# A two-layer streaming encoder trunk on one core: who normalises the second head of each latent attention unit

## The reference, cut to what matters

```python
s = (einsum('bqhl,bkl->bhqk', q_lat, c_kv) + einsum('bqhr,bkr->bhqk', q_rope, k_rope)) * MLA_SCALE
visible = (k_pos[None, :] // CHUNK) <= (q_pos[:, None] // CHUNK)      # CHUNK = 64
p = softmax(where(visible, s, -inf), axis=-1)
o = einsum('bhqk,bkl->bqhl', p, c_kv)
```

## Time and profile before

| | |
|---|---|
| median of three executions | 1850.35 us (1850.24 to 1850.81) |
| the profiled execution | 1849.15 us |
| its span in the profile | 1847.4 us |
| instructions | 33704 |
| TensorE busy | 1824.8 us (99%) |
| VectorE busy | 923.5 us (50%) |
| ScalarE busy | 559.5 us (30%) |
| GpSimd busy | 1075.4 us (58%) |
| granted TensorE clock | 1.0 of full in both attention stages |

### The profile page before, as it was taken

The page is one execution under the profiler, slowest core; times in us unless marked ns, Lnnn a source line. Parts: engine busy times, 40 slices in busy tenths (PEclk is TensorE's granted clock), DMA queues, the critical chain, the costliest instruction groups (busy, mean ns, idle before and its releaser), DMA issues.

```text
span 1847.4 us, 33704 instructions
## 1 busy us (share of the span) xinstructions
PE 1824.8 (99%) x14214; PEld 1768.4 (96%) x14214; DVE 923.5 (50%) x1634; ACT 559.5 (30%) x1197; POOL 1075.4 (58%) x996
## 2 busy tenths in 40 slices
PE   9999999999999999999999999999999999999999
PEld 8999889999999999999999998899999999999999
DVE  6666775232755532523556767752336555235143
ACT  4444443112422211202344445430133222112021
POOL 8686534656555555557665864446456555555564
PEclk9999999999999999999999999999999999999999
DMA  5242112233222222223343421222422222222222
GB/s 189 88 132 86 54 42 84 88 120 112 72 90 92 84 89 92 86 80 97 99 143 93 127 87 47 70 66 84 152 81 75 86 92 89 84 92 91 79 86 95
DMA packets 76231, 170.49 MB, mean 92 GB/s; under 512 B 6384, under 2 KB 34160, under 8 KB 76080
## 3 DMA queue, kind: packets, MB, share of 16 engines
q1 hardware_dynamic: 68752, 160.79, 27.1%
q10 hardware_dynamic: 7328, 7.54, 1.2%
HBM read 156.41 MB, written 9.79 MB: 90 GB/s over the span
## 4 chain that ended last, share of the span: by engine, by line
PE 92%; DVE 5%; ACT 1%; POOL 1%; issue 1%; DMA 0%; SPq 0%; DVEq 0%; ACTq 0%; POOLq 0%
PE ps L1579 76%; PE ps L1614 3%; PE ps L1742 2%; PE ps L1700 2%; DVE xn L1101 1%; DVE xT L1446 1%; DVE mix L1443 1%; PE ps L1796 1%; PE ps L1653 1%; PE ps L1802 1%; DVE R L1101 1%; PE ps L1719 1%; DVE xT L1264 1%; PE ps L1668 1%; PE ps L1738 1%
## 5 line engine op out<-in xcount | busy, mean ns | idle before, releaser
L1579 PE MATMUL ps<-xn,wsp 128*128 128x272 f32 x7824 | 1002.0, 289 | 5.7 <-issue 2.2
L1579 PEld LDWEIGHTS ps<-xn,wsp 128*128 128x128 f32 x7824 | 986.1, 189 | 10.8 <-issue 6.0
L616 POOL CAST wsp<-raw 128x1024 fp32r<-128x1024 f32 (+2 forms) x222 | 220.1, 997 | 505.0 <-DMA raw<-in_wstream 450.3
L623 POOL TENSOR_TENSOR wsp<-raw,wsp 128x1024 fp32r<-128x1024 f32 (+2 forms) x278 | 492.1, 1782 | 16.2
L1579 PE MATMUL ps<-R,wsp 128*128 128x272 f32 x3840 | 486.2, 288 | 0.1
L1579 PEld LDWEIGHTS ps<-R,wsp 128*128 128x128 f32 x3840 | 482.7, 188 | 1.2 <-DVE xT L1130 0.5
L610 POOL TENSOR_TENSOR wsp<-raw,wsp 128x256 fp32r<-128x256 f32 x304 | 235.5, 795 | 12.2
L605 POOL CAST wsp<-raw 128x512 fp32r<-128x512 f32 x152 | 112.2, 738 | 147.9 <-DMA raw<-in_wstream 113.3
L1101 DVE SCALAR_TENSOR_TENSOR R<-ps,R 64x256 fp32r<-64x256 f32 (+12 forms) x264 | 130.0, 510 | 73.2 <-ACT R L753 24.6
L1462 DVE TENSOR_TENSOR mix<-ps,rstd 128x272 f32<-128x272 f32 x88 | 38.8, 441 | 202.9 <-PE ps L1579 192.6
L986 ACT ACTIVATE mix<-vv 128x2 f32<-128x2 f32 x88 | 17.9, 204 | 363.0 <-DVE mix L1464 363.0
(11 more groups left out here) (230 smaller groups left out, 1529.2 us busy)
## 6 DMA issues: line engine op xcount, KB each, us to landing
raw<-in_wstream SPq DMA_DIRECT2D x233, 512.0 KB, 3.5
raw<-in_wstream SPq DMA_DIRECT2D x48, 128.0 KB, 2.6
raw<-in_wstream SPq DMA_DIRECT2D x16, 384.0 KB, 3.0
raw<-in_kc SPq DMA_DIRECT2D x8, 512.0 KB, 3.8
raw<-in_vc SPq DMA_DIRECT2D x8, 512.0 KB, 4.8
xT<-in_x_in SPq DMA_DIRECT2D x8, 272.0 KB, 5.3
out_k_out<-mix ACTq DMA_DIRECT2D x8, 272.0 KB, 2.9
xT<-in_x_in SPq DMA_DIRECT2D x1, 2176.0 KB, 9.2
```

Of the source, the lines that this page charges most:

```text
L616: ins = nc.gpsimd.tensor_copy(dst[:, 0, f], part[:, f])
L623: ins = nc.gpsimd.tensor_tensor(dst[:, 1, f], part[:, f], dst[:, 0, f].bitcast(F32), ALU.subtract)
L1579: mm = pe.matmul(z[:, h], w[:, x, (k0 + k) * P:(k0 + k + 1) * P], rhs[:, y, k, h * HT:(h + 1) * HT], start=(k == 0 and (x, y) == (0, 0)), ...
```

## The change

The first head is normalised by VectorE as before. For the second head VectorE makes the reciprocal alone and raises `p_scaled`; ScalarE, which has just made the exponents, waits for that and writes the head's normalised exponents itself, with a `Copy` whose scale is the reciprocal. In all it counts three steps of `p_scaled` a unit in place of two, and TensorE's waits are renumbered. The M units are as they were but for the count.

```diff
@@ exponents (ScalarE), after the two Exp
+                        act.wait_ge(S["p_scaled"], 3 * (s - NS) + 2)
+                        ac(pr_view(s, w)[:, 1], z_view(s, w)[:, 1], ACT.Copy, scale=rsum[:, 2 * i + 1:2 * i + 2]).then_inc(S["p_scaled"], 1)
@@ normalise (VectorE), M unit
-                                            ALU.mult).then_inc(S["p_scaled"], 2)
+                                            ALU.mult).then_inc(S["p_scaled"], 3)
@@ normalise (VectorE), m unit
-                        for r in range(2):
-                            dve.wait_ge(S["e_done"], 2 * (s - NS) + r + 1)
-                            link(v.reciprocal(rsum[:, 2 * i + r:2 * i + r + 1], rsum[:, 2 * i + r:2 * i + r + 1]))
-                            v.tensor_scalar(pr_view(s, w)[:, r], z_view(s, w)[:, r], rsum[:, 2 * i + r:2 * i + r + 1], None,
-                                            ALU.mult).then_inc(S["p_scaled"], 1)
+                        dve.wait_ge(S["e_done"], 2 * (s - NS) + 1)
+                        link(v.reciprocal(rsum[:, 2 * i:2 * i + 1], rsum[:, 2 * i:2 * i + 1]))
+                        v.tensor_scalar(pr_view(s, w)[:, 0], z_view(s, w)[:, 0], rsum[:, 2 * i:2 * i + 1], None,
+                                        ALU.mult).then_inc(S["p_scaled"], 1)
+                        dve.wait_ge(S["e_done"], 2 * (s - NS) + 2)
+                        v.reciprocal(rsum[:, 2 * i + 1:2 * i + 2], rsum[:, 2 * i + 1:2 * i + 2]).then_inc(S["p_scaled"], 1)
@@ turn (TensorE)
-                            pe.wait_ge(S["p_scaled"], 2 * (n - NS) + 2)
+                            pe.wait_ge(S["p_scaled"], 3 * (n - NS) + 3)
-                                pe.wait_ge(S["p_scaled"], 2 * (n - NS) + r + 1)
+                                pe.wait_ge(S["p_scaled"], 3 * (n - NS) + (3 if r else 1))
```

## The result

The changed kernel takes 1856.95 us (median of six, 1855.58 to 1858.31) where the kernel before, measured beside it, takes 1850.30 (1850.02 to 1851.57). The ratio is 1.0035, 95% interval 1.0025 to 1.0045: slower by 6.6 us. Measured once more with the experiments it was 1855.42 and 1855.98 against 1850.39, ratios 1.0026 (1.0016 to 1.0036) and 1.0025 (1.0012 to 1.0038), so 5.0 to 5.6 us. Forecast were 3.25 us, so 1853.6, in a range that ended at 1855.2. The side was right, the size too small.

What follows compares the result with a forecast made beforehand. TensorE, busy 1824.8 of 1847.4 us, was taken as the bound, so only its waits count. A 2.22 + B 1.03 + C 0 = 3.25 us over the median of 1850.35 gave 1853.6 us, range 1850.9 to 1855.2.

Steps and rivals of the forecast that it cites:

- A: Steps 27 and 28: late value tile vv 1 makes TensorE wait at pv, 1.11 us a layer, 2.22 together.
- B: Steps 20 to 23: scores of step 23 start late, 0.45 us in layer 0 and 0.58 in layer 1, 1.03 together.
- The walk: All 16 units of a layer reckoned by latest input; three tight places, 3.25 us in all, chance 0.60.
- the first bank wait: Step 22: the ql tile waits for the bank ot holds, 216.35 for 216.19; B without the collision is 0.5.
- that first shift: Step 20: the kv eviction puts the chain back by 0.6 us; claimed swallowed in layer 0 by GpSimd holding line 1301.
- The second head's probabilities are ready at the same moment: Every changed unit: probabilities ready at the same moment or up to 0.1 us sooner, no TensorE wait, worth nothing.
- C: Step 29, kv 3: 0.55 us a layer later but covered by the wait for GpSimd, so 0; uncovered 1.1 us.
- The sum: A 2.22, B 1.03 and C 0 give 3.25 us of added TensorE waits.
- Hidden: Rival: TensorE feels nothing, as copies are cheaper or VectorE, with less work, catches up; 1850.4 us, chance 0.14.
- Slower: Rival: GpSimd holds the port through both subtractions, B 2.4 us, 1855.0 us; chance 0.12 including lost cover in C.
- the copy's price: ScalarE's new copy, priced like a sigmoid with scale: 0.48 us at 256 columns, 0.58 at 384, 0.69 at 512.

Runs made afterwards that it cites:

- e5: Changed kernel, but VectorE scales the second head again while ScalarE still waits for the second reciprocal at the same place; 1851.81 us, ratio 1.0004.
- r_after_2: Repeat of the changed kernel with nothing altered, profiled again; 1855.98 us, ratio 1.0025.
- e6: Changed kernel, but in step 22 VectorE writes the maxima to PSUM and the multiplication reads them there; 1855.42 us, ratio 1.0024.
- e3b: Kernel before, with ScalarE's copy in steps 20, 21, 22, 27 and 28 alone, 10 copies of 32; 1855.67 us, ratio 1.0028.
- e4: Changed kernel, with each of the 32 copies placed behind its step's evictions in ScalarE's queue; 1851.20 us, ratio 1.0003.
- e11: Changed kernel, with weight tiles CR 1 and CR 0 exchanged in the stream; 1855.64 us, ratio 1.0026 to the kernel before.
- r_before_1: Repeat of the kernel before with nothing altered, profiled; 1851.24 us, ratio 1.0003 against itself.
- e7: Kernel before, with three tiles moved to other steps (vv 1 to 27, kv 3 to 26, ot 1 to 23); 1857.06 us.
- e8: Changed kernel, with vv 1 moved to step 27, kv 3 to 26 and ot 1 to 23; 1859.50 us.
- e9: Changed kernel, with ScalarE's copy behind the evictions and weight tiles CR 1 and CR 0 exchanged; 1847.39 us, ratio 0.9980 to the kernel before.
- e10: Kernel before, with weight tiles CR 1 and CR 0 exchanged in the stream; 1848.06 us, ratio 0.9986.

## Why the prediction was wrong

**A** was right in mechanism and order, and 16% short: 1.32 us a layer for 1.11. The chain itself came out as reckoned: the exponents 0.63 late and the low parts of `vv` 1.57 late, both beyond the 1.75 us by which TensorE was behind already, the copies 0.474 and 0.581 us in the mean for 0.48 and 0.58. But TensorE started 0.26 us after the low part had ended, and not 0.05 as at lines 1799 and 1805. In e5 the same instruction started 0.26 us late too. Line 1745 has several waits in front of it; but in step 22 it started 0.09 us after its last input. The cause stays open.

**B**, the chain from step 20 to step 23, is the step that failed: 2.65 us where the prediction had 1.03 (2.5 and 2.0 in the two later profiles). Three things in it:
- The walk stopped at the scores of step 23. The `ql` tile of step 22 holds the bank of the next `pv` 0. I had the first bank wait, `ot` before `ql`, inside the sum, but not the one that follows, 0.49 and 0.48 us. It is there in all three profiles of the changed kernel, and in `r_after_2` it is the whole miss: up to the scores of step 23 that profile has 0.52 and 0.49 us, for 0.45 and 0.58 predicted.
- "In layer 0 that first shift is swallowed, since line 1301 was held there by GpSimd anyway." It was swallowed in `r_after_2` and not in the two others. In the first profile the multiplication came at 212.00, at the same moment as GpSimd's next cast, and was held for 0.63 us more. The chain of step 21 was late by that in layer 0 as well.
- "The second head's probabilities are ready at the same moment ..., and TensorE doesn't wait for them." That holds in 15 of 16 units of a layer. In unit 21 the slack was nothing (the scale ended at 215.55, the transposes began at 215.63), and where the chain was late the transposes lost 0.30 and 0.23 us.

**C** was right: the wait of line 1802 grew by 0.55 us, fell under GpSimd's, and cost nothing. Without the cover it costs 0.56, for 0.55 reckoned.

**The sum** of the waits is 5.3 us for 3.25 in the first profile, which alone makes 1855.6 and is past the end of the range. The rest of the first measurement goes with the clock. Of 128 executions of the kernel before, those with a mean granted clock of 1.000 had a median of 1850.2, those of 0.999 1851.2, those of 0.998 1852.4; of 18 of the changed one 1855.0, 1856.6 and 1857.9 (one more, of 1857.2, has a mean of 0.956, which its time doesn't show; it stays unexplained). At an equal clock the difference is 4.8 to 5.5 us. In the first measurement five of six executions of the changed kernel were below 1.000, which fits its 6.6. I had taken the first profile, with its clock at full throughout, for the typical execution.

**The rivals.** "Hidden" was wrong, and its ground, that the queues are short of work, was the very trap: VectorE was idle in the steps where it was late. "Slower" came nearest in time but not by its mechanism: in step 22 line 1303 was held until the end of one GpSimd instruction (217.61 to 218.26 and 0.50 us in layer 1), not through both. The Trainium skill, page "SBUF — State Buffer", section "SBUF: two separate sides", says that whoever starts first holds the shared pair for the whole instruction; all of 0.63, 0.65 and 0.50 us agree with it, and e6 shows that a source in PSUM takes VectorE out of it. As to the copy's price, the Trainium skill's cycles on the page "VectorE: DVE Perf Modes", section "The TRN2 errata — SBUF-src ops pay a fixed extra latency per instruction", gave 0.46 us at 384 columns; the trace has 0.581, and the measurement decides.

## What to carry to other kernels

Where engines work in a written order, moving an instruction onto an idle engine is a question of its place in that queue: put it behind what others wait for, and it is free, as here; ahead of it, it costs up to its own length and its wait in every step that has less slack than that. Look at each unit of a pattern, at the smallest slack and not at the mean, and follow a delay through the PSUM banks as well, to the tile after the next. A wait that hides another should be priced before it is relied on, and it may be the better thing to remove.

## What the runs showed of the hardware that I had not expected

- The clock. A stretch of a little over 3 us at 1.2 GHz right behind the waits of steps 28 to 30 costs 1.4 to 1.5 us, as much as the longest wait ahead of it, and it comes in some executions only. It was there in the profiles of e3b (both layers), e4, e11, r_after_2 and r_before_1, out of 18; e7 and e8 have one at 1162 us, behind their wait for a bank of 2.3 and 2.5 us. With the wait for GpSimd gone the scatter is gone as well: e9 ranges over 1.0 us and e10, but for one execution, too, where the kernel before ranges over 2.8 to 3.6. Yet five executions of e10 and seven of e9 have a mean of 0.999. In the one of these that was profiled (e10) the stretch lay at 877 us, behind the longer gap at the residual, where later waits took it up: the lead over the kernel before is 0.80 us ahead of it and 0.79 behind. So a stretch costs time or not by where it falls. That e10 gained 2.5 us by its median where its waits account for 1.6 fits this.
- A multiplication of two columns on VectorE, 0.22 us by itself, took up to 0.81 when GpSimd's splitting had the port, and when both came at the same moment (212.00) it was GpSimd that went first. Called in the middle of a GpSimd instruction, it ended 0.02 us after that one; called in the last 0.1 us of one, it was in some cases held through the next one as well (211.26 to 212.02 in the kernel before), never longer.
- A per-partition scale costs ScalarE 0.09 us, as the sigmoid had suggested: 0.687 us for 512 columns from PSUM with it, 0.602 without.
